# Cross attention starts after four of its eight query products, and two gate accumulations move to the out-projection

## The reference, cut to what matters

```python
def cross_attention(h, mem_n, wq, wk, wv, wo):      # 4 heads of 256, 256 memory rows
    q = (h @ wq).reshape(bsz, seq, X_HEADS, X_HEAD_DIM)
    k = (mem_n @ wk).reshape(bsz, m_len, X_HEADS, X_HEAD_DIM)
    v = (mem_n @ wv).reshape(bsz, m_len, X_HEADS, X_HEAD_DIM)
    s = jnp.einsum('bqhd,bkhd->bhqk', q, k).astype(jnp.float32) * (X_HEAD_DIM ** -0.5)
    p = jax.nn.softmax(s, axis=-1)
    o = jnp.einsum('bhqk,bkhd->bqhd', p.astype(v.dtype), v).reshape(bsz, seq, D_MODEL)
    return o @ wo
...
def second_block(x, c, ...):                          # two layers l
    c_act = jax.nn.silu(c)
    mod = c_act @ w_ada[l] + b_ada[l]
    shift, scale, gate = jnp.split(mod, 3, axis=-1)   # gate: 1024 numbers for each layer
    ...
    x = x + gate[:, None, :] * rmsnorm(y, g_post[l])
```

## Time and profile before

| what | value |
|---|---|
| median of 3 runs | 1820.02 us (1818.64 to 1822.27) |
| profiled execution | 1820.39 us, span 1819.1 us |
| TensorE busy, share of the span | 1653.1 us, 91% |
| VectorE, ScalarE, GpSimd busy | 727.4, 478.0, 317.5 us |
| mean granted TensorE clock | 0.944 of full speed |
| eight query products to the first out-projection product | 442.11 to 540.05 us of the span |
| expert stage with weight loads back to back | about 650 to 1110 us |

### The profile page before, as it was taken

How to read it: one execution, slowest core, us unless ns; L and a number is a source line. 1 busy time by engine, 2 the same in 40 slices (tenths; PEclk the granted TensorE clock), 3 DMA queues, 4 the chain that set the end, 5 groups by cost and what they waited for, 6 DMA issues and landing times.

```text
span 1819.1 us, 15312 instructions
## 1 busy us (share of the span) xinstructions
PE 1653.1 (91%) x5832; PEld 814.8 (45%) x5832; DVE 727.4 (40%) x1519; ACT 478.0 (26%) x979; POOL 317.5 (17%) x312
## 2 busy tenths in 40 slices
PE   6999999999989699898887787999989999998898
PEld 3544446645454333333333333444455554445553
DVE  2626634254152312111100111459875143996622
ACT  2013242101130010000000001566365134645631
POOL 0000000000000112111101100148143012742500
PEclk9899999999999799898898998989999999899999
DMA  8321032356262599999999998401102130020101
GB/s 322 139 93 46 1 116 93 139 185 236 69 248 87 220 365 408 407 401 409 402 399 403 407 415 325 178 1 70 69 1 88 46 110 0 7 109 24 47 1 46
DMA packets 70960, 324.30 MB, mean 178 GB/s; under 512 B 9290, under 2 KB 12626, under 8 KB 58464
## 3 DMA queue, kind: packets, MB, share of 16 engines
q1 hardware_dynamic: 63552, 308.03, 43.6%
q0 software_dynamic: 6016, 10.51, 1.8%
q10 hardware_dynamic: 1312, 4.72, 0.7%
HBM read 318.95 MB, written 12.67 MB: 182 GB/s over the span
## 4 chain that ended last, share of the span: by engine, by line
PE 68%; DMA 19%; DVE 9%; ACT 2%; issue 2%; POOL 0%; SPq 0%; ACTq 0%; DVEq 0%; POOLq 0%
PE bank L187 65%; DMA arena<-in_w 15%; DMA arena<-h_rows,arena 3%; DVE arena L2454 1%; DVE arena L1214 1%; DVE arena L2438 1%; PE bank L2053 1%; PE bank L567 1%; DVE arena L2495 1%; DVE arena L2508 0%; PE bank L875 0%; DMA arena<-in_params 0%; PE bank L2000 0%; PE bank L662 0%; DVE bank L2486 0%
## 5 line engine op out<-in xcount | busy, mean ns | idle before, releaser
L187 PE MATMUL bank<-arena 128*128 128x512 f32 (+11 forms) x4964 | 1548.0, 551 | 90.6 <-DMA arena<-in_w 53.2
L187 PEld LDWEIGHTS bank<-arena 128*128 128x128 f32 (+3 forms) x4964 | 710.4, 181 | 858.9 <-issue 789.5
L2669 POOL TENSOR_TENSOR arena<-arena 128x512 f32<-128x512 f32 x180 | 205.4, 1141 | 224.1 <-ACT arena L2279 206.6
L1763 POOL TENSOR_TENSOR arena<-arena 128x1 f32<-128x1 f32 (+2 forms) x44 | 32.4, 738 | 682.3 <-DVE arena L1204 456.9
L1711 DVE TENSOR_TENSOR arena<-arena,bank 64x512 f32<-64x512 f32 x32 | 22.1, 691 | 314.2 <-ACT arena L1170 314.2
L2279 ACT ACTIVATE arena<-arena 128x512 f32<-128x512 f32 x180 | 125.9, 717 | 19.6 <-POOL arena L2669 19.3
L959 ACT COPY arena<-bank 128x512 f32<-128x512 f32 (+3 forms) x114 | 60.8, 540 | 228.4 <-PE bank L187 147.3
L1170 ACT ACTIVATE arena<-bank 64x512 f32<-64x512 f32 x32 | 18.9, 591 | 379.6 <-PE bank L187 379.6
L1784 POOL DMA_INDIRECT y_rows<-arena x32 | 32.1, 1004 | 413.4 <-PE bank L875 272.6
L1705 DVE COPY arena<-bank 128x512 f32<-128x512 f32 x32 | 22.1, 692 | 115.2 <-PE bank L875 115.2
L1214 DVE SCALAR_TENSOR_TENSOR arena<-arena 128x512 f32<-128x512 f32 x84 | 63.2, 752 | 3.0
(11 more groups left out here) (264 smaller groups left out, 876.6 us busy)
## 6 DMA issues: line engine op xcount, KB each, us to landing
arena<-in_w SPq DMA_DIRECT2D x96, 2048.0 KB, 34.7
arena<-in_w_in SPq DMA_DIRECT2D x15, 2048.0 KB, 10.8
arena<-in_w_ada SPq DMA_DIRECT2D x12, 2048.0 KB, 8.7
arena<-in_w_out SPq DMA_DIRECT2D x6, 2048.0 KB, 7.7
arena<-in_w_xk SPq DMA_DIRECT2D x2, 2048.0 KB, 9.3
arena<-in_w_xv SPq DMA_DIRECT2D x2, 2048.0 KB, 8.6
arena<-in_w_xq SPq DMA_DIRECT2D x2, 2048.0 KB, 9.9
arena<-in_w_xo SPq DMA_DIRECT2D x2, 2048.0 KB, 9.1
```

Source lines behind the costliest of these rows:

```text
L187: i = pe.e.matmul(o, l, r, start=first and j == 0, stop=last and j == len(pairs) - 1)
L2669: pool.e.tensor_tensor(yc, yc, k.prod[l][n % 4], ALU.add).then_inc(*k.pool.step("sum", l, f, j))
```

## The change

TensorE issues `qx 0..3` and gate (0,0), and then enters the ticks. `qx 4 + tick` stands at the end of ticks 0 to 3, and gate (0,1) at the end of tick 6. The single wait for `qx 7` is replaced by a wait for `qx 2h+1` ahead of each `xs s`. ScalarE's copies of `qx 4..7` stand at the end of the same ticks. VectorE has gate (0,1) at the end of tick 7, and `ada(1,2,0)` behind the last tick. Gate (1,0) and `ada(1,2,1)` are moved into the out-projection, behind the first router turn. GpSimd takes the root of token tile 0 before it waits for gate (1,0). SyncE's list isn't changed, but the events that it waits for move with the work.

```diff
@@ pe_cross
-    for n in range(2):
-        pe.wait_ge(*R.landed(("w_xq", n)))
-        for f in range(4):
-            pe_by_feature(k, pe, ("qx", 4 * n + f), A, R.at(("w_xq", n), 8, 512), f, k.HT)
-        pe_gate(k, pe, 0, n)
-    pe.wait_ge(*A.done("qx", 7))
+    pe.wait_ge(*R.landed(("w_xq", 0)))
+    for f in range(4):
+        pe_by_feature(k, pe, ("qx", f), A, R.at(("w_xq", 0), 8, 512), f, k.HT)
+    pe_gate(k, pe, 0, 0)
+    pe.wait_ge(*R.landed(("w_xq", 1)))
     for tick in range(7 + 6):
         for s, phase in live(tick, 8, 1, 5):
             h, v = divmod(s, 2)
             if phase == 0:
                 b = B.take(pe, A, "xs", s)
+                pe.wait_ge(*A.done("qx", 2 * h + 1))
...
-    pe_gate(k, pe, 1, 0)
+        if tick < 4:
+            pe_by_feature(k, pe, ("qx", 4 + tick), A, R.at(("w_xq", 1), 8, 512), tick, k.HT)
+        elif tick == 6:
+            pe_gate(k, pe, 0, 1)
@@ pe_router
     pe_router_turn(k, pe, 0)
+    pe_gate(k, pe, 1, 0, ROUTER_BANKS)
     pe_out(k, pe, "w_xo", k.OT, [(1, 1), (2, 0)])
@@ act_cross
-    for f in range(8):
-        act.wait_ge(*P.done("qx", f))
-        act.e.activation(k.QX[:, f, :], B.at("qx", f), ACT.Copy, scale=1.0 / 16).then_inc(*A.step("qx", f))
+    for f in range(4):
+        act_qx(k, act, f)
...
+        if tick < 4:
+            act_qx(k, act, 4 + tick)
@@ dve_cross
     dve_ada(k, dve, 0, 2, 1, k.gacc)
-    dve_gate(k, dve, 0, 1)
-    dve_ada(k, dve, 1, 2, 0, k.gacc)
     for tick in range(7 + 6):
...
-    dve_gate(k, dve, 1, 0)
-    dve_ada(k, dve, 1, 2, 1, k.gacc)
+        if tick == 7:
+            dve_gate(k, dve, 0, 1)
+    dve_ada(k, dve, 1, 2, 0, k.gacc)
@@ dve_router
         if t < 3:
             dve_router_turn(k, dve, t)
+        if t == 0:
+            dve_gate(k, dve, 1, 0)
+            dve_ada(k, dve, 1, 2, 1, k.gacc)
@@ pool_first
     for l, n in GATES[1:]:
+        if (l, n) == (1, 1):
+            pool_root(k, pool, k.f_ss[:, 0:1], "f", 0)
         pool.wait_ge(*V.done("gg", *GATES[2 * l + n - 1]))
         pool_gate_rows(k, pool, l, n)
-    for t in range(4):
+    for t in range(1, 4):
         pool_root(k, pool, k.f_ss[:, t:t + 1], "f", t)
```

More of the change, by code:

```diff
@@ L1078, in act_squares, with act_qx @@
     act.e.activation(junk, k.X[:, t, :], ACT.Square, accum_out=ss[:, t:t + 1]).then_inc(*k.act.step("sq", tag, t))
+def act_qx(k, act, f):
+    act.wait_ge(*k.pe.done("qx", f))
+    act.e.activation(k.QX[:, f, :], k.banks.at("qx", f), ACT.Copy, scale=1.0 / 16).then_inc(*k.act.step("qx", f))
 def act_cross(k, act):
```

## The result

The changed kernel took 1813.46 us, the median of 20 runs (1809.6 to 1820.2), and the kernel before 1818.97 us, the median of 20 (1815.59 to 1822.27). The ratio is 0.997, with a 95% interval from 0.9961 to 0.9979: 5.5 us faster, between 3.8 and 7.1. Predicted were 1813.3 us, in a range of 1810.5 to 1818.5.

What follows compares the result with a forecast made beforehand. The prediction took TensorE to bound the span up to the expert stage, there the weight stream, which shifts with TensorE. Savings of 3.67 + 2.91 + 0.11 = 6.69 us off 1820.0 gave 1813.3 us, range 1810.5 to 1818.5.

Steps and rivals of the forecast that it cites:

- the weight stream shifts rigidly: Expert stage: loads from `w1 2` on wait for TensorE events, so an earlier out-projection end moves the whole stream equally.
- Rival 3: Expert stage: the weight stream sets its end by itself, so the gain is hidden; 1820 us, 9% chance.
- The gap: TensorE's idle time ahead of `xt 0`, behind the query products: all 3.67 us were to go.
- The half clock: Ticks behind the gap, `xt 0` to `xt 2`: full clock gives 4.80 us in place of 7.71, saving 2.91 us.
- Rival 2: Ticks behind `qx 7`: the half-clock spell moves there, among short waits, costing 2.9 us; 1816.2 us, 13% chance.
- Gate (1,0): End of the ticks: moving its product saves 0.97 us, 0.86 come back behind the first router turn, net 0.11 us.
- The covers: Slack hiding moved work: 1.9 us ahead of `xt 6`, 1.5 us ahead of the second router turn, `w_xo` landing before use.
- Rival 4: Out-projection waits for the late second half of `w_xo`, 15 us at a 41.4 us landing; 1828 us, 4% chance.

Runs made afterwards that it cites:

- late: The changed kernel with 32 more 128x512 records (13.8 us, result unused) ahead of the first out-projection product; ratio 1.003 to the kernel before.
- gates_only: The changed kernel with all eight query products ahead of tick 0 again, VectorE's new order and moved gates kept; ratio 0.9976 to the kernel before.
- filler: The kernel before with 8 more 128x512 records (3.44 us, result unused) in the idle gap ahead of `xt 0`; ratio 0.9992 to the kernel before.
- half_filler: The kernel before with 4 more 128x512 records (1.72 us, result unused) in the gap ahead of `xt 0`; ratio 0.9988 to the kernel before.
- gate_back: The changed kernel with gate (1,0) and `ada(1,2,1)` back behind tick 12, `ada(1,2,0)` staying behind the ticks; ratio 1.0008 to the kernel before.
- further: The changed kernel with tick 8's `xv` products ahead of `xt 5` and gate (0,1)'s product behind tick 12; ratios 0.9962 and 0.9958 to the kernel before.

## Why the prediction was right

*What bounds the kernel.* The claim that the weight stream shifts rigidly held, and late measured it: 14.1 us for 13.8, in one profile of a stage whose length varies by 4 us. Rival 3 (the gain is hidden) falls with it, as far as that scatter lets one see.

*The gap.* Right in cause: VectorE's block ahead of the first row maximum, as gates_only shows. It was mis-sized by 0.3 us. I took the 3.67 us that stand in brackets, but these count from the modelled end of the last matmul, and the next one can start ahead of that end. By starts, 132 records of 0.43 and four scores of 1.74 us are 63.7 us, and `xt 0` came 67.70 us after the first query product: 3.98 us were lost.

*The half clock.* 2.91 us were forecast; filler and half_filler measured 2.87 alone. Rival 2, the clock that swings among short waits, didn't come: the rows of 516 to 520 and 530 to 532 have 1.00. So the rule of the Trainium skill that was weighed there, in "TensorE: Matmul & The Clock Gate", section "A second HAM failure mode: psum-queue depth-cycling", isn't borne out by these ticks, with waits of 1.02 and 0.68 us. What that section tells of is a bf16 kernel, and this one is float32.

*Gate (1,0).* Forecast a net 0.11 us. From the last record's issue the first product came 0.83 us later (529.73 to 530.56), not 0.93, and before it was 1.04: 0.21 us net. With 3.98 and 2.87 that is 7.06 us, and T2 lost 7.03.

*The covers* all held: `xt 6` has no wait, the second router turn none, with 1.67 us to spare where 1.5 were worked out, and `w_xo` none, whose second half was issued at 504.08, 26 us ahead of its use. Rival 4, the late landing, didn't appear.

*The total.* 6.7 us were forecast, the stage lost 7.0, and three sets of runs say 5.5 (3.8 to 7.1), 6.2 (2.7 to 9.6) and 8.6 (5.8 to 11.1). That the median of 1813.46 us lies 0.2 us from the forecast 1813.3 is luck in part: the kernel before ran at 1818.97 us beside it, 1.05 us under the 1820.02 from which the forecast started, and the gain was 5.5 us and not 6.7. Of the nine measurements of kernels that got shorter in T2, seven gained less in total than in T2, each within or near its interval; whether a small part is lost behind the stage stays open.

What my text didn't see is that half of the change does all of it. It put the end of the gap down to the query products in the ticks, and gates_only loses the gap without them. It asked what the interleaving hides and what the moved gates free, but not each without the other; the sum came out right because the gap is gone either way.

## What to carry to other kernels

When TensorE waits for a short first item of a pipeline, look at what stands ahead of that item in the other engine's list: here 7 us of unrelated VectorE work had slipped in between, and moving it was enough, once gate (1,0), which waits for a part of it, had moved too (left in its old place it cost 8.07 us in gate_back). Look also at what that work itself waits for: VectorE had stood idle for 21.05 us ahead of it. Before two edits are made for one gap, work out what each does alone. And price an idle gap with its clock: 3.98 us of wait cost 6.85 us, and 1.72 us of useless matmuls inside it brought 2.87 us back.

## What the runs showed of the hardware that was not expected

- Idle times of 3.67 us (before) and 4.98 us (gate_back) in the stage of the change were each followed by a spell at the lower clock level, which cost 2.9 and 2.7 us; 0.68, 0.87, 1.02 and 1.97 us were not (1.97 in a single profile).
- The length of a wait alone doesn't tell when the clock falls. In the router, all twelve profiles have a wait of 3.1 us behind short products with waits of 0.5 and 1.4 us between them, at which the clock falls to 0.50. This is the row of the changed kernel:

```profile
607.71 1.12 PE L187 MATMUL bank<-arena 128*128 128x64 f32 x4 [3.14 <-DVE arena L1590]
```

  By the stretches of 2 us (0.52 over 606 to 608) the clock fell about 1.5 us into that wait. In further, with the same products and waits, 604 to 606 us has 0.68 and the next stretch 0.50, so it fell about 0.2 us into the wait that begins at 604.51.
- Single profiles of the changed kernel agree to 0.02 us over the 143 us of the stage around the change, but the first query product, ahead of which the programs don't differ, came anywhere between 438.3 and 443.8 us, and the expert stage took 467.7 to 471.8 us. In the changed kernel's first profile 1.6 of the 8.7 us by which the span fell were won ahead of the change. What makes this scatter was not tried.
